# A two-layer retention and short-convolution trunk: the convolution computed with tokens on partitions instead of channels

## The reference, cut to what matters

```
for each of 2 layers:
  h = RMSNorm(x) * norm_pre * (1 + scale(c)) + shift(c)          # 256 tokens x 2048
  z = h @ w_in                                                   # 2048 x 14336
  gb, gcin, u, g_c, q, k, v, g_r = split(z)
  y_conv = gb * conv3(gcin * u) * silu(g_c)
  y_ret  = GroupNorm(retention(rope(q), rope(k), v)) * gn_gain * silu(g_r)
  o = concat(y_conv, y_ret) @ w_out                              # 4096 x 2048
  x = x + gate(c) * RMSNorm(o) * norm_post

conv3(cu)[s] = w[2]*cu[s] + w[1]*cu[s-1] + w[0]*cu[s-2]          # causal, per channel, zeros before token 0
```

## Time and profile before

| | |
|---|---|
| Time, three runs | median 1734.82 us (1734.46 to 1735.0) |
| The profiled execution | 1733.56 us, of it 1731.7 us between first and last instruction |
| Granted TensorE clock, mean | 0.997 |
| PE busy | 98% |
| DVE busy | 66% |
| ACT busy | 42% |
| POOL busy | 2% |
| Moved from memory | 411.28 MB, 239 GB/s over the span |

### The profile page before, as it was taken

The page is one execution under the profiler, slowest core; times in us unless marked ns, Lnnn a source line. Parts: engine busy times, 40 slices in busy tenths (PEclk is TensorE's granted clock), DMA queues, the critical chain, the costliest instruction groups (busy, mean ns, idle before and its releaser), DMA issues. The chain is left out here.

```text
span 1731.7 us, 19009 instructions
## 1 busy us (share of the span) xinstructions
PE 1696.0 (98%) x7771; PEld 1385.5 (80%) x7771; DVE 1135.0 (66%) x1307; ACT 730.8 (42%) x832; POOL 38.1 (2%) x78
## 2 busy tenths in 40 slices
PE   6899999999999999999999999999999999999998
PEld 3567888888888888888878888888888888888886
DVE  2798766878787776677776545555554555467776
ACT  3444444433444444343354443444444444443332
POOL 4000000000000000000000000000000000000000
PEclk9999999999999999999999999999999999999999
DMA  9998545687878767777765555555555555568775
GB/s 342 383 378 309 190 165 195 250 290 267 298 267 291 282 230 241 270 273 280 282 235 170 177 194 188 177 179 192 195 176 193 184 185 172 190 230 303 281 282 190
DMA packets 227399, 414.62 MB, mean 239 GB/s; under 512 B 7520, under 2 KB 48880, under 8 KB 226544
## 3 DMA queue, kind: packets, MB, share of 16 engines
q1 hardware_dynamic: 225888, 408.97, 68.2%
q10 hardware_dynamic: 1424, 4.43, 0.6%
HBM read 411.28 MB, written 2.10 MB: 239 GB/s over the span
## 5 line engine op out<-in xcount | busy, mean ns | idle before, releaser
L766 DVE TENSOR_TENSOR w_lo<-stage,w_hi 128x1024 fp32r<-128x1024 f32 x574 | 692.8, 1222 | 509.8 <-ACT w_hi L570 507.2
L570 ACT CAST w_hi<-stage 128x1024 fp32r<-128x1024 f32 x574 | 596.0, 1051 | 937.5 <-PE Z L1186 610.9
L1184 PE MATMUL Z<-w_hi,H 128*128 128x512 f32 x1784 | 704.0, 395 | 12.1 <-DVE w_lo L766 8.4
L1186 PE MATMUL Z<-w_hi,H 128*128 128x512 f32 x1784 | 696.5, 390 | 0.0
L1185 PE MATMUL Z<-w_lo,H 128*128 128x512 f32 x1784 | 695.6, 390 | 0.0
L1184 PEld LDWEIGHTS Z<-w_hi,H 128*128 128x128 f32 x1784 | 335.6, 188 | 88.7 <-issue 14.2
L1186 PEld LDWEIGHTS Z<-w_hi,H 128*128 128x128 f32 x1784 | 335.6, 188 | 71.0
L1185 PEld LDWEIGHTS Z<-w_lo,H 128*128 128x128 f32 x1784 | 336.0, 188 | 68.0
L787 DVE SCALAR_TENSOR_TENSOR acc<-stage,c_silu,acc 128x512 f32<-128x512 f32 x240 | 180.1, 751 | 6.8
L1184 PE MATMUL Z<-w_hi,YC 128*128 128x512 f32 x256 | 102.3, 399 | 0.0
L1184 PE MATMUL Z<-w_hi,YR 128*128 128x512 f32 x256 | 100.5, 393 | 0.0
(11 more groups left out here) (149 smaller groups left out, 697.6 us busy)
## 6 DMA issues: line engine op xcount, KB each, us to landing
stage<-in_w_in SPq DMA_DIRECT2D x186, 1024.0 KB, 5.1
stage<-in_w_ada SPq DMA_DIRECT2D x64, 1024.0 KB, 7.4
stage<-in_w_out SPq DMA_DIRECT2D x64, 1024.0 KB, 7.4
stage<-in_w_in SPq DMA_DIRECT2D x74, 512.0 KB, 5.4
front_stage<-in_w_ada SPq DMA_DIRECT2D x32, 1024.0 KB, 11.2
xt<-in_x SPq DMA_DIRECT2D x2, 1024.0 KB, 6.5
dec<-decay SPq DMA_DIRECT2D x8, 256.0 KB, 5.5
rows<-in_b_ada ACTq DMA_DIRECT2D x2, 1024.0 KB, 8.0
```

Of the source, the lines that this page charges most:

```text
L570: N.copy(w_bufs(n, h)[0], stage[:, slot_of(n), 2 * h:2 * h + 2, :]).then_inc(s_hi, 1)
L766: V.tensor_tensor(lo, stage[:, slot_of(n), 2 * h:2 * h + 2, :], hi.bitcast(F32), ALU.subtract)\
L1184: T.matmul(z[:, i, :], hh, wh, start=ch.first and a == 0, stop=False)
L1186: ins = T.matmul(z[:, i, :], hl, wh, start=False, stop=stop)
```

## The change

`cu` stays in token layout. Two shifted copies of it, one and two tokens later, are made by DMA from SBUF to SBUF, since a shift by tokens is now a shift by partitions. Each copy is made by three DMAs: partitions 0 to 111 of the source, the rest up to the last partition but one (or two), and the last one (two) tokens of tile 0, which go to the first partitions of tile 1. GpSimd writes zeros to the tokens before the first (step on POOL, two memsets a turn). The taps, which are now along the free dimension, come as rows of 512 numbers sent to all 128 partitions, three DMAs a turn, issued by ACT at step 13 (turn 0: step 2); the moves are issued by ACT at step 22 (turn 0: step 9).

DVE does the convolution in token layout with five operations on 128x1024 (`conv_tap`): at the first step of `tap` one multiplication, at the second and third one multiplication and one addition each. The gate is formed as before; DVE then multiplies it by the convolution still in token layout, and only this product is transposed by PE (8 pieces of 128x128 a turn), one step later than the gate was before (step 30; in turn 0 step 21, as before). ACT and DVE form the two parts of `YC` from the PSUM buffer. PE's transposes of `cu`, ACT's `y0` and DVE's eight operations of `conv` are gone.

```diff
 USUAL = Steps_at(rope=5, radd=6, trq=6, qkt=8, v=9, scores=7, p=9, inner=9, stats=11, sgr=13, yn=13, mult=14,
-                 tr=14, yrhi=16, yrlo=17, gcopy=17, cu=21, trc=21, y0=23, conv=24, sg=25, gate=29, trg=29,
-                 ymul=31, yhi=32, ylo=33)
+                 tr=14, yrhi=16, yrlo=17, gcopy=17, cu=21, back=22, tap=(22, 24, 25), sg=25, gate=29,
+                 ymul=30, trg=30, yhi=32, ylo=33)
 FIRST = Steps_at(rope=2, radd=3, trq=4, qkt=6, v=3, scores=6, p=8, inner=9, stats=11, sgr=7, yn=13, mult=13,
-                 tr=17, yrhi=19, yrlo=20, gcopy=99, cu=8, trc=9, y0=11, conv=12, sg=9, gate=10, trg=21,
-                 ymul=23, yhi=24, ylo=25)
+                 tr=17, yrhi=19, yrlo=20, gcopy=99, cu=8, back=9, tap=(9, 11, 12), sg=9, gate=10,
+                 ymul=15, trg=21, yhi=23, ylo=24)
...
+MOST = 112
...
         @block.scalar
+                    if s == (at.yn if t else 2):
+                        if t == 0:
+                            act.wait_ge(s_ga, len(FRONT_GROUPS))
+                        else:
+                            act.wait_ge(s_cv, t)
+                        j = t % TURNS
+                        for k in range(CONV_K):
+                            row = conv_w[t // TURNS, k, j * BLK:(j + 1) * BLK]
+                            dst = taps[j][:, k, :] if j < TURNS - 1 else v_sb[:, k, :] if k < 2 else acc2[:, :]
+                            act.dma_start(dst, row.partition_broadcast(P)).then_inc(s_taps, 16)
...
-                    if s == at.y0:
-                        act.wait_ge(s_trc, t + 1)
-                        act.wait_ge(s_in, t + 1)
-                        if t:
-                            act.wait_ge(s_ylo, t)
-                        for e in range(TILES):
...
-                            ins = N.activation(R4[:, e, :], cu_bank(t)[:, e, :], ACT.Copy, scale=prm[:, w:w + 1])
+                    if s == at.back:
+                        act.wait_ge(*taken(t, UU))
+                        act.wait_ge(s_zero, t + 1)
+                        cu, b = cu_buf(t), behind_buf(t)
+                        for n_back in (1, 2):
+                            to = b[:, n_back - 1, :, :]
+                            moved = s_back[n_back - 1]
+                            act.dma_start(to[n_back:n_back + MOST, :, :], cu[0:MOST, :, :]).then_inc(moved, 16)
+                            act.dma_start(to[n_back + MOST:P, :, :], cu[MOST:P - n_back, :, :]).then_inc(moved, 16)
+                            act.dma_start(to[0:n_back, 1, :], cu[P - n_back:P, 0, :]).then_inc(moved, 16)
...
         @block.vector
+            def conv_tap(t, n_back):
+                row, b = tap_row(t, CONV_K - 1 - n_back), behind_buf(t)
+                if n_back == 0:
+                    dve.wait_ge(s_taps, 16 * CONV_K * (t + 1))
+                    dve.wait_ge(s_in, t + 1)
+                    if t:
+                        dve.wait_ge(s_trg, t)
+                    dve.wait_ge(*taken(t, UU))
+                    me.then(V.tensor_tensor(tok(R4), cu_buf(t), row, ALU.mult))
+                    return
+                at_ = b[:, n_back - 1, :, :]
+                dve.wait_ge(s_back[n_back - 1], 48 * (t + 1))
+                me.then(V.tensor_tensor(at_, at_, row, ALU.mult))
+                me.wait()
+                ins = V.tensor_tensor(tok(R4), tok(R4), at_, ALU.add)
...
-                    if s == at.conv:
-                        dve.wait_ge(s_y0, t + 1)
-                        for back in (1, 2):
-                            for e in range(TILES):
...
+                    for n_back in range(CONV_K):
+                        if s == at.tap[n_back]:
+                            conv_tap(t, n_back)
                     if s == at.gate:
...
-                            dve.wait_ge(s_trc, t + 1)
+                            dve.wait_ge(s_cv, t + 1)
                     if s == at.ymul:
-                        dve.wait_ge(s_trg, t + 1)
+                        dve.wait_ge(*taken(t, GB))
                         dve.wait_ge(s_cv, t + 1)
-                        V.tensor_tensor(R4[:, :, :], gate_bank(t), R4[:, :, :], ALU.mult).then_inc(s_ym, 1)
+                        V.tensor_tensor(tok(R4), gate_buf(t), tok(R4), ALU.mult).then_inc(s_ym, 1)
...
         @block.gpsimd
+            def zeros(t):
+                for n_back in (1, 2):
+                    ins = G.memset(behind_buf(t)[0:n_back, n_back - 1, 0, :], 0.0)
...
         @block.tensor
-                    if s == at.trc:
-                        pe.wait_ge(*taken(t, UU))
...
-                        turned(cu_bank(t), cu_buf(t)).then_inc(s_trc, 1)
                     if s == at.trg:
-                        pe.wait_ge(*taken(t, GB))
+                        pe.wait_ge(s_ym, t + 1)
...
-                        turned(gate_bank(t), gate_buf(t)).then_inc(s_trg, 1)
+                        turned(gate_bank(t), tok(R4)).then_inc(s_trg, 1)
```

More of the change, by code:

```diff
@@ L136 @@
 Steps_at = namedtuple("Steps_at", "rope radd trq qkt v scores p inner stats sgr yn mult tr yrhi yrlo"
-                      " gcopy cu trc y0 conv sg gate trg ymul yhi ylo")
+                      " gcopy cu back tap sg gate ymul trg yhi ylo")
 USUAL = Steps_at(rope=5, radd=6, trq=6, qkt=8, v=9, scores=7, p=9, inner=9, stats=11, sgr=13, yn=13, mult=14,
-                 tr=14, yrhi=16, yrlo=17, gcopy=17, cu=21, trc=21, y0=23, conv=24, sg=25, gate=29, trg=29,
-                 ymul=31, yhi=32, ylo=33)
+                 tr=14, yrhi=16, yrlo=17, gcopy=17, cu=21, back=22, tap=(22, 24, 25), sg=25, gate=29,
+                 ymul=30, trg=30, yhi=32, ylo=33)
 FIRST = Steps_at(rope=2, radd=3, trq=4, qkt=6, v=3, scores=6, p=8, inner=9, stats=11, sgr=7, yn=13, mult=13,
-                 tr=17, yrhi=19, yrlo=20, gcopy=99, cu=8, trc=9, y0=11, conv=12, sg=9, gate=10, trg=21,
-                 ymul=23, yhi=24, ylo=25)
+                 tr=17, yrhi=19, yrlo=20, gcopy=99, cu=8, back=9, tap=(9, 11, 12), sg=9, gate=10,
+                 ymul=15, trg=21, yhi=23, ylo=24)
 ALL_TURNS = LAYERS * TURNS
+MOST = 112
 def base(t):
@@ L286, in build @@
         front_stage, _ = place("front_stage", [P, SLOTS, CK, BLK], F32, at_yr)
+        taps = [place(f"taps{j}", [P, CONV_K, BLK], F32, at_yr + 4 * 2 * S * 4 * (j + 1) + (0 if j else 4 * 2 * S * 4))[0]
+                for j in range(TURNS - 1)]
+        behind = [place(f"behind{j}", [P, 2, NT, BLK], F32, at_yc + 4 * 2 * S * 4 * j)[0] for j in range(TURNS)]
+        behind_0, _ = place("behind_0", [P, 2, NT, BLK], F32, at_yr + 4 * 2 * S * 4)
         c_cols, _ = place("c_cols", [P, KT, COL], F32, at_r4)
@@ L357, in build @@
         s_cu = sem("cu_done")
-        s_trc = sem("cu_transposed")
-        s_y0 = sem("conv_last_tap")
+        s_taps = sem("conv_taps_loaded")
+        s_zero = sem("first_tokens_zeroed")
+        s_back = [sem(f"cu_moved_back{n}") for n in (1, 2)]
         s_cv = sem("conv_done")
@@ L458, in p_buf, with behind_buf, tap_row @@
             return at[:, 0:2 * 3 * P].rearrange("p (h s) -> p h s", h=2)
-        def cu_bank(t):
-            return four(A if t == 0 else B)
+        def behind_buf(t):
+            return behind[t % TURNS] if t else behind_0
+        def tap_row(t, k):
+            row = taps[t % TURNS][:, k, :] if t % TURNS < TURNS - 1 else v_sb[:, k, :] if k < 2 else acc2[:, :]
+            return row.rearrange("p (o f) -> p o f", o=1).broadcast_to([P, NT, BLK])
         def gate_bank(t):
@@ L708, in _ @@
                         act.wait_ge(s_in, t)
+                        if t == TURNS:
+                            act.wait_ge(s_cv, t)
                         N.copy(v_sb[:, :, :], z_of(t, VV)).then_inc(taken(t, VV)[0], 1)
@@ L752, in _ @@
                     if s == at.yhi:
-                        act.wait_ge(s_ym, t + 1)
-                        N.copy(YC[:, 4 * (t % TURNS):4 * (t % TURNS) + 4, 0:S], R4[:, :, :]).then_inc(s_yhi, 1)
+                        act.wait_ge(s_trg, t + 1)
+                        N.copy(YC[:, 4 * (t % TURNS):4 * (t % TURNS) + 4, 0:S], gate_bank(t)).then_inc(s_yhi, 1)
             squares(1, NB - 1)
@@ L873, in x_end @@
                 variance(xsq[:, i, :], NT + i)
+            def conv_tap(t, n_back):
[13 more added lines that the diff above has]
+                ins = V.tensor_tensor(tok(R4), tok(R4), at_, ALU.add)
+                if n_back == CONV_K - 1:
+                    ins.then_inc(s_cv, 1)
+                else:
+                    me.then(ins)
             def front_rows(k, kc):
@@ L1133, in _ @@
             pool.sem_inc(s_tab, 1)
+            def zeros(t):
+                for n_back in (1, 2):
+                    ins = G.memset(behind_buf(t)[0:n_back, n_back - 1, 0, :], 0.0)
+                    if n_back == 1:
+                        me.then(ins)
+                me.wait()
+                ins.then_inc(s_zero, 1)
+            pool.wait_ge(s_ga, len(FRONT_GROUPS))
+            zeros(0)
             for t in range(ALL_TURNS):
                 pool.wait_ge(s_mv, t + 1)
+                if t:
```

(6 more changed lines are left out.)

21 lines of the change are left out of this document (3 added, 18 removed).

## The result

| | before | changed kernel |
|---|---|---|
| Median, 7 runs each | 1734.65 us (1733.55 to 1735.0) | 1740.49 us (1737.6 to 1741.59) |
| Ratio, 95% interval | | 1.0032 (1.0023 to 1.0042) |
| The profiled execution | 1733.56 us, span 1731.7 | 1741.59 us, span 1739.7 |

The kernel became 5.8 us slower, 6.5 us above the forecast and outside its range.

The account below looks back on a forecast made before the run. PE's stream of matmuls was taken to bound the kernel. The turns' terms, 2.2 + 1.9 - 0.3 - 4.6 = -0.8 us, on the median of 1734.82 gave 1734.0 us, range 1730.4 to 1738.6.

Parts of the forecast that it names:

- What leaves PE: PE's eight transposes of cu and the slower half behind them go: 0.92 us a turn, 7.3 us over eight turns.
- What comes to DVE: Five added DVE operations for eight removed, 2.7 us more a turn, ACT's nine issues (0.44 each), covered in quiet turns.
- The taps are issued nine steps before their use. ... These cost nothing: The taps' loads, like the zeros on GpSimd, come in time before their use and cost nothing.
- Turn 2: Chunks 88 and 89: PE waits 0.6 us behind DVE's taps but is 0.9 earlier; -0.3 us, ends -0.9 and +1.
- turns 3 to 7: No conditioning loads at these steps, so PE's saving is kept: 5 x -0.92 = -4.6 us, ends -4.6 and -3.
- a rival (1739.6, 9 in 100): Copies hold up chained weight loads, chunk 58's by 5.1 us, and the same at turn 2: +4.8, 1739.6; 9 in 100.
- Turn 0: First tap at chunk 37 waits for s_in: PE waits 2.6 us before chunk 38, 0.4 before 41; +2.2 us.
- a rival at 10 in 100: Granted clock falls after the new 2.6 us wait in turn 0, costing 1.7 us: 1735.3 us; 10 in 100.
- Turn 1: Chained loads, chunks 55 to 69: copies delay chunk 58's load 1.5, chunk 66 adds 0.4; +1.9 us, ends 0 and +3.5.
- The delay d: Delay of chunk 58's weight load by the copies in turn 1: between 0 and 2.7 us, taken as 1.5.
- Not spread over the 16 engines: Each copy runs on one DMA engine, not 16: 17 us a turn, about 1870 us; 2 in 100.
- Full gain, 1727.5: All of PE's saving is kept, which needs DVE not to wait at chunk 37: 1727.5 us; 4 in 100.

Follow-up runs that it names:

- the kernel without the three causes: Changed kernel without turn 0's wait for s_in, the taps' broadcasts and the copies' DMAs (tap values and shifts left out): 1727.37 us, ratio 0.9957.
- the first experiment: Changed kernel, but turn 0's first tap no longer waits for s_in (the retention's products): 1735.52 us, ratio 1.0004.

## Why the prediction was wrong, step by step

**What leaves PE: right.** 0.92 us a turn. In turns 4 to 7 the starts show -3.6 for four turns, and the kernel without the three causes came out 7.2 below the one before.

**What comes to DVE: right** that its own length costs nothing in quiet turns. ACT's queue was undersized: six issues took 0.59 to 1.46 us each in turn 1, 4.9 in sum where I took 0.44 each; quiet turns cover that too.

**"The taps are issued nine steps before their use. ... These cost nothing": this step failed.** I asked whether the transfers would arrive in time and not what they would hold up. Turn 2's taps stand beside a weight load that the earlier trace rows would give 5.1 us and that took 7.5 before and 11.9 after. Turn 3's stand among conditioning loads that I had not looked at: "turns 3 to 7 have no conditioning loads at these steps" holds for the steps of the convolution and not for step 13. I priced such a delay only for the copies in turn 1, and my 0.6 before chunk 89 came from DVE's work alone. I had the mechanism as a rival (1739.6, 9 in 100), with the copies as its cause. Turn 2 came out 4.0 us above its term (1.6 of it the clock, which fell behind the wait before chunk 89) and turn 3 2.0: 6.0 of the 8.8 us between forecast and measurement in the traces. With the broadcasts away all of it is gone; in turn 2 the copies have a part in it, as the table of the five kernels shows (the experiment with none of the three).

**Turn 0: the wait right, its price too low.** Forecast 2.6 us for chunk 38, measured 2.51; DVE idle for 11.2, forecast 11. No second wait came at chunk 41, but the clock fell, which I had left to a rival at 10 in 100: 1.6 us for the 1.7 expected there. One of the two marks between which I placed the new wait, the 2.09 us with the clock at 1.00 behind it, was no mark: behind the same wait in the changed kernel's trace, 2.07 us, the granted clock of 51 to 59 us is 0.79. Turn 0 came out 1.3 above its term.

**Turn 1: right within 0.3, but by luck.** The errors cancel. The delay d of chunk 58's load was 2.9, outside my upper end of 2.7, where I took 1.5. Of that, 1 us fell on the lateness that PE already had from turn 0 (the first experiment gives it back), and 0.99 us came back at chunk 65. The rule of alternating queues in the Trainium skill ("DMA: Bandwidth & Descriptors", section on queues, rings and completion order) gave an estimate of 2.3, nearer than mine.

**Front and output projection: +1.5 not forecast.** +0.8 lies in the first 15 chunks, which the change does not reach. It is the scatter of executions: the eight experiments' kernels, alike in this stretch, stand there between -0.5 and +1.2 against the trace of before. The clock has its part in it; between 95 and 105 us the granted clock is 0.73 in the changed kernel's trace and 0.83 in that of before. The +0.8 in the output projection of layer 0 comes back as +0.1 to +0.6 in every experiment with the new computation, also where all the DMAs are gone, and is 0.0 in the kernel before with the DMAs. So it belongs to the new computation and not to the transfers; where in it was not followed up.

**The rivals.** "Not spread over the 16 engines" did not happen with the division and did without it. "Full gain, 1727.5" is what the kernel without the three causes gave, 1727.37.

## What to carry to other kernels

Ask of each added DMA two things: does it land in time, and which load that something waits for lies beside it; near a chain of loads the second decides, and moving the same broadcasts to another place made 4.8 us here with the same work. A wait placed ahead of an operation holds everything behind it in that engine's queue, so compare what it waits for with how far that engine runs ahead. When several small costs meet, take each away alone and then all together, and compare stretch by stretch: the last kernel gives what the change is worth, and the stretches show which costs exist only where two causes meet.

## What the runs showed that I had not expected

- **The clock.** After a wait of about 2 us it sometimes fell and sometimes did not. It fell behind 2.51 us (0.64 in the rows above), behind 1.95 us before chunk 89 and behind 2.24 us in the kernel before with the DMAs; each time about 1.5 us were lost. It did not fall behind 1.92 us before chunk 61, nor at chunk 38 behind 2.45 us in the kernel without the taps' broadcasts and behind 2.51 us in the one without the copies. The windows at chunk 89 of the changed kernel, and at chunk 38 of the kernel without the copies:

```profile
549.00:553.00 4.00, 3.28 (x10) 2.65 (x11) 3.93 (x5) 1.68 (x2) 0.00 (x0) 0.74 1.07 381
553.00:557.00 4.00, 4.00 (x16) 3.22 (x16) 3.96 (x5) 1.36 (x2) 0.00 (x0) 0.83 0.60 188
```
```profile
246.00:250.00 4.00, 4.00 (x19) 3.27 (x19) 4.00 (x4) 1.05 (x1) 0.00 (x0) 1.00 0.47 143
```

So the length of the wait does not decide. The front, where the kernels are alike, shows it best: behind the wait of 2.07 to 2.12 us before chunk 5 the granted clock of 51 to 59 us is 0.79 in six traces and 1.00 in three, the kernel before among them. What decides is open. It may be a part of why the changed kernel's seven runs spread over 4 us: their mean granted clocks go from 0.993 to 0.996, three of the four longest runs have 0.993 and the two shortest 0.996, but one of 1741.25 us has 0.996 too. That is a hint and was not tested.

- **Copies from SBUF to SBUF** of 448 KB landed in 3.6 us in the median, in turn 1, beside loads, in 6.8. A copy of the last one token is 2 KB, and its issue is as long as that of a large one (0.59 us in turn 1). The last issue of the six took 1.46 us in turn 1 and 1.32 in turn 2, beside loads, and 0.65 or 0.66 in the six other turns.
- **Weight loads beside the other queue** took 12.0 us (chunk 58's) and 11.9 (turn 2) for 1 MB, where the same loads took 9.2 and 7.5 in the kernel before; the median of such loads is 5.3. With the undivided copies, the two weight loads of this size issued between 1093 and 1124 us, while the first copy of turn 4 was under way, took 13.3 us in the median.
